# Four low halves on GpSimd, two moved subtractions, a two-matmul square sum in tile 0, and the mask ahead of a product in a one-core hybrid attention and recurrence block

## What is computed

```
h = rmsnorm(x, w_norm_pre)
q_a, k_a, v_a, z_a, q_r, f_r, i_r, z_r = split(h @ w_in)
o_a = window_sink_attention(rope(q_a), rope(k_a), v_a, sinks) * silu(z_a)
f = lb + (1 - lb) * sigmoid(f_r);  G = cumsum(log f) in chunks of 64
A = where(causal, (q_r * exp(G)) @ ((1 - f) * exp(-G)).T, 0)
o_r = A @ i_r + (q_r * exp(G)) @ state        # the state runs from chunk to chunk
o_r = rmsnorm(o_r, hgrn_norm) * silu(z_r)
out = x + rmsnorm(concat(o_a, o_r) @ w_out, w_norm_post)
```

## Time and profile before

| | us |
|---|---|
| median of 3 runs | 864.01 |
| lowest, highest | 863.54, 865.32 |
| time of the profiled execution | 862.26 |
| its span | 860.5 |
| TensorE busy in it | 847.7 |
| VectorE, ScalarE, GpSimd busy | 634.0, 524.7, 131.0 |

### The profile page before, as it was taken

One profiled execution on the slowest core, in us unless ns is written; L12 is line 12 of the kernel. 1 busy time (PEld: TensorE's weight loads), 2 busy tenths in 40 slices (PEclk: granted clock), 3 DMA queues, 4 the chain that ended last, 5 costly groups with the idle time before them and its releaser, 6 DMA issues.

```text
span 860.5 us, 12473 instructions
## 1 busy us (share of the span) xinstructions
PE 847.7 (99%) x4404; PEld 696.6 (81%) x4404; DVE 634.0 (74%) x1141; ACT 524.7 (61%) x1041; POOL 131.0 (15%) x110
## 2 busy tenths in 40 slices
PE   8999999999999999999999999999999999999997
PEld 7787788888878778888888878888888877888885
DVE  6878878674576899879754679887775478988846
ACT  7766445773576658677546455965843655576544
POOL 0000013430310100353200000144300000004220
PEclk9999999999999999999999999999999999999999
DMA  9699994838999896546997454545799674444586
GB/s 323 223 326 401 326 323 165 341 147 309 416 372 416 283 329 222 196 172 212 354 399 276 177 196 172 171 164 205 252 371 397 229 266 147 148 147 162 188 324 255
DMA packets 62797, 225.88 MB, mean 263 GB/s; under 512 B 6992, under 2 KB 7248, under 8 KB 62672
## 3 DMA queue, kind: packets, MB, share of 16 engines
q1 hardware_dynamic: 58048, 205.56, 64.9%
q0 software_dynamic: 4112, 18.88, 6.7%
q10 hardware_dynamic: 576, 0.66, 0.2%
HBM read 172.63 MB, written 60.82 MB: 271 GB/s over the span
## 4 chain that ended last, share of the span: by engine, by line
PE 61%; DVE 20%; ACT 8%; issue 5%; DMA 3%; SPq 1%; POOL 0%; DVEq 0%; ACTq 0%; POOLq 0%
PE bank L597 42%; PE turn_b L853 4%; PE score_b L853 4%; PE bank L853 4%; DVE kv_tok L1376 4%; DMA kept_lo<-w_lo 2%; ACT probs_t L952 1%; PE score_b L630 1%; DVE q_gate L1465 1%; DVE f_c L1623 1%; DVE s_stats L1423 1%; PE turn_b L654 1%; DMA kept_lo<-t_probs 1%; PE turn_b L707 1%; ACT probs L961 1%
## 5 line engine op out<-in xcount | busy, mean ns | idle before, releaser
L597 PE MATMUL bank<-h_hi,w_lo 128*128 128x512 f32 x832 | 327.3, 393 | 0.0
L597 PE MATMUL bank<-h_lo,w_hi 128*128 128x512 f32 x832 | 326.7, 393 | 0.0
L597 PE MATMUL bank<-h_hi,w_hi 128*128 128x512 f32 x832 | 324.6, 391 | 0.0
L597 PEld LDWEIGHTS bank<-h_lo,w_hi 128*128 128x128 f32 x832 | 156.6, 188 | 34.7 <-issue 3.3
L597 PEld LDWEIGHTS bank<-h_hi,w_lo 128*128 128x128 f32 x832 | 156.5, 188 | 33.1
L597 PEld LDWEIGHTS bank<-h_hi,w_hi 128*128 128x128 f32 x832 | 156.5, 188 | 32.3 <-issue 0.2
L1723 POOL TENSOR_TENSOR mix_lo<-v_r,mix_hi 128x512 fp32r<-128x512 f32 x16 | 21.2, 1325 | 360.4 <-ACT v_r L1143 360.4
L1253 DVE TENSOR_TENSOR w_lo<-w_raw,w_hi 128x1024 fp32r<-128x1024 f32 x36 | 44.7, 1248 | 33.1 <-ACT w_hi L925 32.7
L1376 DVE STREAM_TRANSPOSE kv_tok<-k_mid 32x128 f32<-32x128 f32 x192 | 58.1, 303 | 2.8
L925 ACT ACTIVATE w_hi<-w_raw 128x1024 fp32r<-128x1024 f32 x38 | 39.7, 1050 | 19.0 <-issue 10.6
L1689 POOL TENSOR_TENSOR x_acc<-x_acc,x_sq 128x512 f32<-128x512 f32 x21 | 33.0, 1570 | 68.4 <-ACT x_sq L975 68.4
(11 more groups left out here) (292 smaller groups left out, 1578.8 us busy)
## 6 DMA issues: line engine op xcount, KB each, us to landing
w_hi<-kept_hi SPq DMA_DIRECT2D x114, 512.0 KB, 3.8
w_lo<-kept_lo SPq DMA_DIRECT2D x114, 512.0 KB, 4.9
w_raw<-in_weights SPq DMA_DIRECT2D x38, 512.0 KB, 7.7
kept_hi<-w_hi SPq DMA_DIRECT2D x34, 512.0 KB, 8.3
kept_lo<-w_lo SPq DMA_DIRECT2D x34, 512.0 KB, 9.4
x_in<-in_x_rows SPq DMA_DIRECT2D x8, 1024.0 KB, 8.5
x_in<-in_x SPq DMA_DIRECT2D x15, 512.0 KB, 8.4
t_rows<-in_weights POOLq DMA_DIRECT2D x4, 1024.0 KB, 13.2
```

Source lines behind the costliest of these rows:

```text
L597: mm = pe.matmul(acc(w)[:, :], stationary[:, s, k, :], moving[:, k, :], start=(m == 0), stop=(m == 3 * KT - 1), skip_group_check=True)
```

## The change

Four things are changed. (1) `save_sum` on GpSimd makes the low halves of the weight sums k = 4 to 7 itself, each ahead of its own store; VectorE's `sum_low` is left with k = 0 to 3. (2) The low halves of weight tiles 36 and 37 are made ahead of tile 0's output block b = 3 instead of behind it. (3) Tile 0's square sum is done as in the other tiles: VectorE writes the rounded sum to `mix_hi`, the sum again to `x_acc`, and the difference to `mix_lo`, and TensorE multiplies both. The place of `sum_x` in weight tile 2 is now ahead of matmul 6 in tile 0 (it was 20) and ahead of matmul 20 in tiles 1 to 3 (it was 0). (4) `mask_head` copies the masked scores first and multiplies the carried state behind that.

```diff
@@ -110,6 +110,7 @@
 LAST_STORES = STORES[:-1] + ((1, (0,), 7), (1, (1,), 8))
 PLAIN_STORES = ((0, (0, 1), 1, 1), (1, (0, 1), 3, 0), (2, (0, 1), 4, 2), (3, (0,), 5, 0), (3, (1,), 6, 0))
 SUMS_IN = {(FAST - 1, OUT0): (2, 3), (FAST, 5): (0,), (FAST, 6): (1,), (FAST, 8): (4,), (FAST, 9): (5,), (FAST, 10): (6,), (FAST, 11): (7,)}
+SUMS_POOL = 4
 SUMS_SPLIT = {3 + k: (k,) for k in range(T_TILES)}
 SUMS_OUT = (4, 6, 8, 9, 11, 12, 13, 15)
 SUMS_MADE = {6: (0, None), 7: (1, None), 9: (0, B12), 10: (1, B12), 12: (2, None), 14: (2, B11), 16: (3, None), 17: (3, B21)}
@@ -346,7 +347,7 @@
         t_base, t_high, t_low, t_saved = (sem(n) for n in ("t_base", "t_high", "t_low", "t_saved"))
         t_made = [sem(f"t_made{i}") for i in range(4)]
         t_loaded = [sem(f"t_loaded{i}") for i in range(T_TILES)]
-        probs_saved = sem("probs_saved")
+        probs_saved, t_pool_low = sem("probs_saved"), sem("t_pool_low")
         lo_split = count("lo_split", WT)
         k_mid_done, o_low = count("k_mid_done", HEADS), count("o_low", HEADS)
         p_normed = count("p_normed", PAIRS)
@@ -580,14 +581,10 @@
                     pe.wait_ge(y_read.sem, y_read.after(tile, -4))
                 else:
                     pe.wait_ge(y_posted.sem, y_posted.after(tile, -1))
-                if tile:
-                    pe.wait_ge(x_low, tile)
-                    pe.matmul(sum_b, ones_r[:, :], mix_hi[:, 0, :], start=True, stop=False, skip_group_check=True)
-                    pe.matmul(sum_b, ones_r[:, :], mix_lo[:, 0, :], start=False, stop=True,
-                              skip_group_check=True).then_inc(x_summed.sem, 1)
-                    return
-                pe.wait_ge(x_added.sem, x_added.after(tile, KT - 2))
-                pe.matmul(sum_b, ones, x_acc[:, :], start=True, stop=True).then_inc(x_summed.sem, 1)
+                pe.wait_ge(x_low, tile + 1)
+                pe.matmul(sum_b, ones_r[:, :], mix_hi[:, 0, :], start=True, stop=False, skip_group_check=True)
+                pe.matmul(sum_b, ones_r[:, :], mix_lo[:, 0, :], start=False, stop=True,
+                          skip_group_check=True).then_inc(x_summed.sem, 1)
 
             def products(t, w, m, last):
 
@@ -730,7 +727,7 @@
             def between(t, w, m):
 
                 q, odd = divmod(w - SCORES0, 2)
-                if w == XSUM and m == (0 if t else 20):
+                if w == XSUM and m == (20 if t else 6):
                     sum_x(t)
                 if w == V_TURN and m == 4 and t < DVE_TURN:
                     pe.wait_ge(stored[1], 32)
@@ -1288,7 +1285,11 @@
                     dve.wait_ge(sum_step, k // 2 - 1)
                 dve.tensor_tensor(q_gate[:, 0:2, :], q_gate[:, 0:2, :], q_gate[:, k:k + 2, :], ALU.add).then_inc(sum_step, 1)
             dve.wait_ge(sum_step, KT // 2 - 1)
+            dve.tensor_tensor(mix_hi[:, 0, :], q_gate[:, 0, :], q_gate[:, 1, :], ALU.add).then_inc(sum_step, 1)
             dve.tensor_tensor(x_acc[:, :], q_gate[:, 0, :], q_gate[:, 1, :], ALU.add).then_inc(x_added.sem, x_added.per_tile)
+            dve.wait_ge(sum_step, KT // 2)
+            dve.wait_ge(x_added.sem, x_added.after(0, KT - 2))
+            dve.tensor_tensor(mix_lo[:, 0, :], x_acc[:, :], mix_hi[:, 0, :], ALU.subtract).then_inc(x_low, 1)
             dve.wait_ge(act_setup, 1)
             dve.tensor_tensor(lb_m[:, :], lb_e[:, 0:HEADS], lb_e[:, HEADS:], ALU.add).then_inc(lb_step, 1)
             dve.wait_ge(lb_step, 2)
@@ -1343,10 +1344,10 @@
             def mask_head(t, h):
 
                 dve.wait_ge(a_done.sem, a_done.after(t, h))
+                dve.copy_predicated(by_pair(a_t[:, :]), causal.unsqueeze(1).broadcast_to([P, PAIRS, P]),
+                                    by_pair(head_b[:, :])).then_inc(a_masked.sem, 1)
                 if t:
                     dve.tensor_scalar(read_state[:, 0, :], carry[:, h, :], to_mid[:, h % 2, 0:1], None, ALU.mult)
-                dve.copy_predicated(by_pair(a_t[:, :]), causal.unsqueeze(1).broadcast_to([P, PAIRS, P]),
-                                    by_pair(head_b[:, :])).then_inc(a_masked.sem, 1)
 
             def carry_head(t, h):
 
@@ -1635,8 +1636,9 @@
                             dve.wait_ge(a_sum.sem, a_sum.after(t, 0))
                             sum_head(t, h)
                     for k in SUMS_SPLIT.get(s, ()) if t == FAST else ():
-                        sum_low(k)
-                    for i in splits(t, s) if t or kind not in (0, 1) else ():
+                        if k < SUMS_POOL:
+                            sum_low(k)
+                    for i in splits(t, s) if (t, s) != (1, 0) and (t or kind not in (0, 1)) else ():
                         if i in DVE_LOW:
                             split_lo(i)
 
@@ -1652,6 +1654,9 @@
                     if b == 3 and t + 1 < TILES:
                         dve.wait_ge(x_high, t + 1)
                         dve.tensor_tensor(mix_lo[:, 0, :], x_acc[:, :], mix_hi[:, 0, :], ALU.subtract).then_inc(x_low, 1)
+                    if b == 3 and t == 0:
+                        for i in splits(1, 0):
+                            split_lo(i)
                     copy_y(t, 1, b)
                     if b == 0:
                         dve.wait_ge(res_loaded, t * 32 + 32)
@@ -1677,7 +1682,12 @@
 
             def save_sum(k):
 
-                pool.wait_ge(t_low, k + 1)
+                if k < SUMS_POOL:
+                    pool.wait_ge(t_low, k + 1)
+                else:
+                    pool.wait_ge(t_high, k + 1)
+                    pool.tensor_tensor(t_in[k], t_in[k], t_hi[k].rearrange("p k n -> p (k n)").rearrange("p (k m) -> p k m", m=P), ALU.subtract).then_inc(t_pool_low, 1)
+                    pool.wait_ge(t_pool_low, k + 1 - SUMS_POOL)
                 pool.wait_ge(tile_done.sem, tile_done.after(FAST, SUMS_OUT[k]))
                 rows, saved = slice((WT + k) * P, (WT + k + 1) * P), probs_saved if k < 2 else t_saved
                 pool.dma_start(kept[0][rows, :].rearrange("p (k m) -> p k m", k=2), t_hi[k].bitcast(FP32)).then_inc(saved, 16)
```

## The result

The changed kernel takes 875.31 us (median of 4 runs, 872.56 to 877.40), the kernel before 863.77 on the same chip (4 runs): ratio 1.0129, 95% interval 1.0096 to 1.0162, 11.5 us slower. Forecast were 870.8 us and a range up to 872.8. The direction holds, the size doesn't.

What follows compares the result with a forecast made beforehand. TensorE's own work was taken as the bound, busy 847.7 of 860.5 us. Tile 0 +4.0, tile 1 +3.4 and mask -0.6 gave +6.8, on 864.0 making 870.8 us, range 866.3 to 872.8.

Steps and rivals of the forecast that it cites:

- GpSimd's hold-up: Tile 1's attention: GpSimd's subtractions block VectorE operations with two SBUF operands, 1.6 + 2.2 + 1.2 = 5.0 us.
- the late scale: Tile 1: square sum now ahead of matmul 20, so ScalarE has it, and the first attention gate comes, 3.2 us later.
- Tile 0, +4.0 us: Tile 0's square sum: TensorE stalls 4.6 us for VectorE, weight tile 3 begins at 29.6 instead of 25.61.
- 18 x 0.227: Tile 0, behind the sum: the 18 products left in the weight tile take 0.227 us each, 4.1 us.
- Rival 2: Clock falls in tile 0's stall, products behind it at half rate: at most 2.9 us more, 873.7 us; chance 0.12.
- The price of up to 2.9 us: Cost of a clock fall in tile 0, from the kernel's start, where products stood at half rate for 5.8 us.
- Tile 1, +3.4 us: TensorE leaves tile 1's attention 3.4 us late: 3.2 late scale, less 4.6 saved, plus 5.0 held, less 0.2 waiting.
- 5.0 us for 4 x 1.14 saved: Tile 1: VectorE is held up 5.0 us by GpSimd in exchange for the four low halves it drops.
- Start of tile 1, -1.3: Start of tile 1: TensorE's 1.02 us wait for weight tile 36's low half goes, with a slow restart; 1.0 to 1.5.
- mask, -0.6: Head outputs: four TensorE waits of at most 0.2 us for the mask go, -0.6 us (0 to -0.7).

Runs made afterwards that it cites:

- e4: Changed kernel with tile 0's sum back at matmul 20, tiles 1 to 3's at 0, all subtractions on VectorE: 862.21 us, ratio 0.9995 to the kernel before.
- e7: Kernel of e4 with tile 0's square sum put back at matmul 6: 867.19 us, ratio 1.0046 to the kernel before.
- e9: Kernel of e7 with 16 useless products on TensorE ahead of tile 0's wait: 865.61 us, ratio 1.0029 to the kernel before.
- e13: Kernel of e14 with VectorE's subtraction k=6 of tile 1 moved behind the next step's product g_b: 860.79 us, ratio 0.9984 to the kernel before.
- e6: Kernel of e4 with the square sums of tiles 1 to 3 put back at matmul 20: 866.40 us, ratio 1.0039 to the kernel before.
- e1: Changed kernel with tile 0's square sum back at matmul 20, still in two matmuls: 868.44 us, ratio 1.0075 to the kernel before.
- e8: Kernel before with two edits alone, masking first and tile 1's first low halves ahead of tile 0's last block: 862.10 us, ratio 0.9990.
- e5: Kernel of e4 with GpSimd making the low halves k=4 to 7 again: 866.66 us, ratio 1.0040 to the kernel before.
- e10: Kernel of e5 with GpSimd's subtraction k=5 back on VectorE: 867.73 us, ratio 1.0053 to the kernel before.
- e15: Kernel before with masking first alone: 862.18 us, ratio 0.9996.
- e16: Kernel before with tile 1's first low halves ahead of tile 0's last block alone: 863.11 us, ratio 1.0004.
- e12: Kernel of e14 with VectorE's subtraction k=4 of tile 1 also moved behind the next product g_b: 860.88 us, ratio 0.9970 to the kernel before.
- e14: Kernel of e4 with tile 0's two-matmul square sum at matmul 2 of weight tile 3: 861.52 us, ratio 0.9984 to the kernel before.
- e3: Changed kernel with the square sums of tiles 1 to 3 back at matmul 0: 872.66 us, ratio 1.0103 to the kernel before.
- e2: Changed kernel with all eight subtractions of the weight sums back on VectorE: 872.02 us, ratio 1.0104 to the kernel before.

## Why the prediction was right in direction and too low

- **Which mechanisms.** The three named as costs (tile 0's sum, GpSimd's hold-up, the late scale) were the cost: e4, without them, is back at the time before.
- **Tile 0, +4.0 us.** The start of the sum was right (25.1, measured 24.98). The step that failed is "18 x 0.227", all products at full clock: some eight of them ran at half clock, 1.6 us more (31.24 against 29.6). Alone, the part costs 4.7 us (e7), of which 1.6 to 1.8 are the clock (e9).
- **Rival 2 was the case, with a chance of 0.12.** I held it against this rival that the stall was the shorter one beside 4.7 us. The changed kernel shows half clock behind waits of 2.5, 3.2 and 2.0 us. The yardstick was no bound but one draw: over the profiles of all the kernels here the clock falls 2.0 (e13) to 5.1 us (e6) behind TensorE's last product. The price of up to 2.9 us, taken from the kernel's start (products 0.43 apart there, though the window of the earlier trace rows reads 1.00), was 1.6 in tile 0. I had also counted it for tile 0 alone. Over three places it took 5.9 us by the windows, more than the 4.5 us by which the forecast was short; TensorE's waits by themselves were shorter than forecast, at the first pair 3.2 in place of 3.9, in tile 0 2.5 in place of 4.6. That the total is only 4.5 us off is in part luck: these errors have opposite signs.
- **Tile 1, +3.4 us.** With tile 0's sum taken back to 20 (e1), I had +3.4 - 0.6 = +2.8 against the kernel before; e1 measures +5.8, some 0.4 of that perhaps for tile 0's second matmul form (e4 against e8, within the noise). Of the 2.6 us then missed, 1.5 are clock: e1's stretch from 290 to 295 is busy all its 5.00 us at 0.70. The late `x_scale` itself was sized right: 247.84 is 8.85 later than before, of which 5.6 are TensorE's shift (its product 0 of weight tile 2 starts at 242.65, where it was ready at 237.04), so 3.2 for the 3.2 forecast, and e6 prices it alone at 3.9 with half clock in it. The step that failed beside the clock is "5.0 us for 4 x 1.14 saved", that GpSimd's part nets 0.4: on top of the late sum it costs 2.3 (e1 less e6), alone 4.2 (e5 less e4), of which some 1.5 are clock. The holds come to 5.6 us in the changed kernel (2.3 + 2.8 + 0.4 for k = 4, 5, 6), near the 5.0, so the hold-up was not what was mis-sized; how much of the 4.6 saved reached TensorE no run takes apart.
- **GpSimd's hold-up** was right as a mechanism and nearly as a size: 2.3 us at the quotient and 2.8 at the scan, forecast 1.6 and 2.2. By the Trainium skill (SBUF — State Buffer, Who interferes with whom) the one that issues second is blocked for the other's whole instruction, not slowed; e10's three-element product beside a subtraction of 2.42 us agrees on the length, with 2.59. On the order the traces don't bear it out: in both large holds of the changed kernel and in this one of e10 the recorded start of VectorE's operation is the earlier, by 0.1 to 0.5 us, and it was held all the same. The places were not right: I had k = 4 hold the gate product behind the quotient, it held the quotient; k = 5 the subtraction behind the scan, it held the scan; k = 6 held the three-element product for 0.4 and not 1.2; k = 7 nothing, as said. Such places hang on tenths of a microsecond: in e5 k = 4 held the gate product after all (3.22), and e10 moved one and another appeared.
- **Start of tile 1, -1.3, and mask, -0.6.** The waits did go, as said. As time they are 0.8 us together (e8) in place of 1.9, and nothing measurable each (e15, e16), partly because 0.4 to 0.7 us reappear as wait at the first pair.

## What to carry to other kernels

A stall in a matmul stream may be paid twice (the shortest here that was: 2.0 us): its length, and the products behind it at half clock. If the operand can't come sooner, put the matmul where TensorE arrives as its operand is ready (w = 3, matmul 2 here: e12, e13 and e14, with e8's two edits in them, are 1.1 to 2.3 us faster than before) or fill the wait. Work moved to GpSimd is not free because GpSimd is idle: here one of its subtractions stopped the operation of VectorE with two SBUF operands that stood at that moment, even one of three elements, and which one that was changed from kernel to kernel (the quotient in the changed kernel, the gate product in e5). A producer moved later by 3.2 us, ahead of an unbroken chain of engines, cost 3.9 here (e6), half clock included.

## What the runs showed of the hardware

- Half clock (0.50, 1.2 GHz) stood behind waits of TensorE of 2.5 us in the changed kernel's tile 0 and 4.9 in e7's, 3.2 and 2.7 at turn(0) (the changed kernel and e1; e6), and 2.0 at the last pair (the changed kernel, also e3, e5, e10), most of them far shorter than the 4.7 that I had as a yardstick. In the changed kernel's tile 0 the clock fell only when TensorE had been busy again for a microsecond. The length of the wait alone does not decide: behind 2.0 at the last pair of e1, 2.7 and 2.5 at the first pair of e2 and 2.1 there in e3 and e5 the windows read 1.00. What decides is open. Each time the clock was back within 7 us of its fall. That this makes the times of such kernels scatter is a guess; the mean clocks of the executions fit it, without proof: of e5's twelve (863.81 to 868.18 us) the two slowest have the lowest, 0.994, and one of the two fastest the highest, 0.999 (the other 0.996).
- VectorE's operation with two SBUF operands was held for 2.3 to 2.8 us by a GpSimd subtraction of 2.4 us that began 0.1 to 0.5 us behind the operation's own recorded start, and for 2.0 us by one that began 0.3 us ahead of it (k = 4 in e10). Its duration in the trace is then that of the hold-up and the work together: in the changed kernel, e1, e3, e5 and e10 each ended its usual duration, less 0.1 us, behind the end of the subtraction. Products with one operand in PSUM were not held: beside k = 6 in the changed kernel, from 318.26 to 320.67, this one took its usual time:

```profile
318.79 0.68 DVE L1564 TENSOR_TENSOR v_r<-bank,x_scale 128x512 f32<-128x512 f32 x1
```
